# First norm of a two-block forward pass: the shift enters as one-row products ahead of the transposes, and start-up transfers are asked for in another order

## The reference, cut to what matters

```python
mod = jax.nn.silu(c) @ w_ada[l] + b_ada[l]
shift1, scale1, gate1, shift2, scale2, gate2 = jnp.split(mod, N_MOD, axis=-1)
h = modulate(rms_norm(x, norm1_g[l]), shift1, scale1)     # h * (1 + scale1) + shift1
proj = h @ w_in[l]
```

## Time and profile before

| | us |
|---|---|
| three runs, median | 1350.91 |
| lowest and highest | 1350.15 and 1354.35 |
| the profiled execution | 1351.17 |
| its span from first to last instruction | 1349.4 |
| PE busy | 1214.6 (90%) |
| DVE busy | 554.2 (41%) |
| ACT busy | 452.0 (33%) |

### The profile page before, as it was taken

One profiled execution on the slowest core, in us unless ns is written; L12 is line 12 of the kernel. 1 busy time (PEld: TensorE's weight loads), 2 busy tenths in 40 slices (PEclk: granted clock), 3 DMA queues, 4 the chain that ended last, 5 costly groups with the idle time before them and its releaser, 6 DMA issues.

```text
span 1349.4 us, 16311 instructions
## 1 busy us (share of the span) xinstructions
PE 1214.6 (90%) x6501; PEld 841.4 (62%) x6504; DVE 554.2 (41%) x805; ACT 452.0 (33%) x657; POOL 45.6 (3%) x66
## 2 busy tenths in 40 slices
PE   3799999879799789969999869999989988899998
PEld 0677677765344335424554328888879866688886
DVE  0545545674111112211121146464456654544444
ACT  1345445242111112201222134444445544444443
POOL 1000000000000000000000020020010001000000
PEclk9799999979899889979999979999999978899999
DMA  9986565548999999999999996555525106355540
GB/s 345 374 292 241 217 222 185 209 165 331 376 422 420 393 422 421 421 387 422 421 421 421 417 331 196 187 187 187 198 100 187 63 1 210 122 199 189 187 152 32
DMA packets 115087, 360.03 MB, mean 267 GB/s; under 512 B 14995, under 2 KB 62404, under 8 KB 83980
## 3 DMA queue, kind: packets, MB, share of 16 engines
q1 hardware_dynamic: 113360, 352.71, 69.1%
q10 hardware_dynamic: 1340, 2.94, 0.6%
q0 software_dynamic: 320, 3.46, 0.6%
HBM read 355.89 MB, written 4.50 MB: 267 GB/s over the span
## 4 chain that ended last, share of the span: by engine, by line
PE 80%; DMA 9%; DVE 5%; ACT 3%; issue 1%; POOL 1%; SPq 1%; ACTq 0%; DVEq 0%; POOLq 0%
PE bank L1943 30%; PE bank L2120 16%; PE bank L2047 9%; DMA ring<-in_w_up_e 6%; PE bank L2145 5%; PE bank L1994 5%; PE bank L2097 3%; PE bank L2157 3%; DMA att<-in_buckets 1%; PE bank L2212 1%; DMA raw_g<-in_w_in 1%; PE bank L1959 1%; PE bank L2234 1%; DVE g_lo L1243 1%; PE bank L2036 1%
## 5 line engine op out<-in xcount | busy, mean ns | idle before, releaser
L1243 DVE TENSOR_TENSOR g_lo<-raw_g,g_hi 128x2048 fp32r<-128x2048 f32 (+2 forms) x88 | 201.8, 2295 | 119.1 <-ACT g_hi L798 62.4
L2120 PE MATMUL bank<-ring,xg 128*64 128x512 f32 (+1 forms) x1152 | 211.9, 636 | 41.6 <-DMA ring<-in_w_up_e 41.6
L1943 PE MATMUL bank<-g_hi,xt_hi 128*128 128x512 f32 (+1 forms) x592 | 240.1, 406 | 5.8 <-DVE xt_lo L1859 2.2
L1943 PE MATMUL bank<-g_hi,xt_lo 128*128 128x512 f32 (+1 forms) x592 | 232.7, 393 | 0.0
L1943 PE MATMUL bank<-g_lo,xt_hi 128*128 128x512 f32 (+1 forms) x592 | 232.4, 392 | 0.0
L2120 PEld LDWEIGHTS bank<-ring,xg 128*64 128x64 f32 (+1 forms) x1152 | 65.6, 133 | 184.5 <-issue 184.5
L1943 PEld LDWEIGHTS bank<-g_hi,xt_hi 128*128 128x128 f32 x592 | 113.0, 191 | 35.7 <-issue 10.2
L1943 PEld LDWEIGHTS bank<-g_hi,xt_lo 128*128 128x128 f32 x592 | 112.6, 190 | 24.1
L1943 PEld LDWEIGHTS bank<-g_lo,xt_hi 128*128 128x128 f32 x592 | 112.9, 191 | 21.2
L2145 PE MATMUL bank<-ring,a_t 128*64 128x512 f32 (+1 forms) x576 | 102.2, 597 | 1.4 <-DVE pickT L1346 0.9
L1388 DVE SCALAR_TENSOR_TENSOR arena<-arena,w_row_of,bank 128x256 f32<-128x256 f32 x28 | 13.5, 481 | 218.4 <-ACT arena L918 214.3
(11 more groups left out here) (347 smaller groups left out, 1579.9 us busy)
## 6 DMA issues: line engine op xcount, KB each, us to landing
ring<-in_w_gate_e SPq DMA_DIRECT2D x64, 1024.0 KB, 12.5
ring<-in_w_up_e SPq DMA_DIRECT2D x64, 1024.0 KB, 16.5
ring<-in_w_down_e SPq DMA_DIRECT2D x64, 1024.0 KB, 15.5
raw_g<-in_ffn_w_gu SPq DMA_DIRECT2D x44, 1024.0 KB, 8.5
raw_g<-in_w_in SPq DMA_DIRECT2D x26, 1024.0 KB, 7.0
raw_d<-in_ffn_w_down SPq DMA_DIRECT2D x22, 1024.0 KB, 4.9
ada_d<-in_w_ada SPq DMA_DIRECT2D x16, 1024.0 KB, 5.0
raw_g<-in_w_out SPq DMA_DIRECT2D x8, 1024.0 KB, 5.1
```

The source lines that it names most:

```text
L1243: dve.tensor_tensor(lo, raw, hi.bitcast(F32), ALU.subtract).then_inc(S.lo_g, 1)
L1943: last = pe.matmul(out_, src[s][:, c, b * P:(b + 1) * P], w((g_hi, g_lo)[m], i), start=start and i == 0 and k == 0, stop=stop and i == len ...
L2120: last = pe.matmul(bank(4)[r, :].rearrange("p (g n) -> p g n", g=2), xg[:, s // 2 % 2, c, at_:at_ + r.stop - r.start], gate_up_raw(pair, j ...
```

## The change

The shift is no longer spread and added by DVE. `ada_spread` spreads scale1 alone, into banks 6 and 7. A new `first_transposes` first puts the shift into banks 0 to 3, already transposed: for each of 16 blocks of 128 x 128, two products of one row of `mod_rows` (64 columns of the stationary side) with a row of ones. Then it adds h to them by 16 plain products with the identity, where the old code used transposes. DVE only scales.

The transfers: on ACT's queue `con`, the gain and `g2_rows` are asked for after the third piece of `w_ada` has landed and ahead of the squares of x; the two small tables and `b_ada` come ahead of x. On POOL's queue `t_scratch` waits until group 0 of `w_in` has been split and `n_scratch` until the last group has.

```diff
             pool.wait_ge(tb_sb, 1)
             pool.dma_start(t_one, t_bias).then_inc(in_["t1"], 16)
-            pool.wait_ge(in_["t1"], 16)
-            pool.dma_start(t_dram, t_one.unsqueeze(0).to_broadcast([P, NH, BX])).then_inc(in_["tw"], 16)
-
             link(pool.memset(rpb_pad, 0.0))
...
             pool.dma_start(n_one, rpb_pad).then_inc(in_["n1"], 16)
+            pool.wait_ge(in_["t1"], 16)
+            pool.wait_ge(M.lo_g, 2 * G_WIN + 2)
+            pool.dma_start(t_dram, t_one.unsqueeze(0).to_broadcast([P, NH, BX])).then_inc(in_["tw"], 16)
             pool.wait_ge(in_["n1"], 16)
+            pool.wait_ge(M.lo_g, 2 * (G_WIN + N_WIN - 1) + 2)
             pool.dma_start(n_dram, n_one.unsqueeze(0).to_broadcast([64, NH, NR])).then_inc(in_["nw"], 16)
...
             act.dma_start(c_col, a["c"].rearrange("o (p c) -> p (o c)", c=DC)).then_inc(in_["c"], 16)
-            act.dma_start(con[:, :], a["con"]).then_inc(in_["con"], 16)
-            act.dma_start(x[:, :, :], a["x"].rearrange("o (b p) n -> p (o b) n", p=P)).then_inc(in_["x"], 16)
             act.dma_start(relb_in[0:32, :], a["rel_bias_t"]).then_inc(in_["relb"], 16)
...
-            act.dma_start(gain1, a["norm1_g"].to_broadcast([P, D])).then_inc(in_["g1"], 16)
-            for j in range(2):
-                act.dma_start(g2_rows[32 * j:32 * j + 32, :], a["norm2_g"][:, j * 512:(j + 1) * 512].to_broadcast([32, 512]))\
-                    .then_inc(in_["g2r"], 16)
+            act.dma_start(x[:, :, :], a["x"].rearrange("o (b p) n -> p (o b) n", p=P)).then_inc(in_["x"], 16)
+
+            def late_loads():
+
+                act.wait_ge(landed_ada[2], 16)
+                act.dma_start(gain1, a["norm1_g"].to_broadcast([P, D])).then_inc(in_["g1"], 16)
+                act.dma_start(con[:, :], a["con"]).then_inc(in_["con"], 16)
+                for j in range(2):
...
             act.activation(c_sil, c_col, ACT.Silu).then_inc(c_silu, 1)
+            late_loads()
             squares(0, [x[:, b, :] for b in range(TB)], in_["x"], 16, lambda i: h[:, i, :])
 
-            act.wait_ge(ada_bc, 4)
-            act.activation(shift1, ps[0][:, :, :].rearrange("p a n -> p (a n)"), ACT.Copy).then_inc(ada_ev, 1)
...
-                dve.wait_ge(ada_bc, 4)
-                src = ps[1][:, :, :].rearrange("p a n -> p (a n)")
+                dve.wait_ge(ada_bc, 2)
+                src = ps[3][:, :, :].rearrange("p a n -> p (a n)")
...
             for b in range(TB):
-                link(scaled(h[:, b, :], x[:, b, :], b, gain1))
-                dve.wait_ge(ada_ev, 1)
-                dve.tensor_tensor(h[:, b, :], h[:, b, :], shift1, ALU.add).then_inc(h_ready, 1)
+                scaled(h[:, b, :], x[:, b, :], b, gain1).then_inc(h_ready, 1)
...
+            def first_transposes():
+
+                def block(q, i):
+                    return bank(q)[:, i * P:(i + 1) * P]
+
+                for q in range(4):
+                    for i in range(4):
+                        for j in range(2):
+                            row = mod_rows[32 * j:32 * j + 1, 4 * (q % 2) + i:512:DC]
+                            pe.matmul(block(q, i)[64 * j:64 * j + 64, :], row, ones[32 * j:32 * j + 1, :],
+                                      start=i == 0, stop=False, skip_group_check=True)
+                pe.wait_ge(in_["con"], 16)
+                for q in range(4):
+                    pe.wait_ge(h_ready, q // 2 + 1)
+                    for i in range(4):
+                        ins = pe.matmul(block(q, i), h[:, q // 2, 4 * (q % 2) + i:D:DC], ident,
+                                        start=False, stop=True, skip_group_check=True)
+                    ins.then_inc(M.xt_ps, 1)
```

More of the change, by code:

```diff
@@ L352, in build @@
         landed_ada_d = [sem("landed_ada_d0"), sem("landed_ada_d1")]
-        ada_used, ada_rows, ada_bc, ada_ev = sem("ada_used"), sem("ada_rows"), sem("ada_bc"), sem("ada_ev")
+        ada_used, ada_rows, ada_bc = sem("ada_used"), sem("ada_rows"), sem("ada_bc")
         tb_ps, tb_sb = sem("tb_ps"), sem("tb_sb")
@@ L783, in _ @@
                     .then_inc(in_["bada"], 16)
-            act.dma_start(gain1, a["norm1_g"].to_broadcast([P, D])).then_inc(in_["g1"], 16)
-            for j in range(2):
-                act.dma_start(g2_rows[32 * j:32 * j + 32, :], a["norm2_g"][:, j * 512:(j + 1) * 512].to_broadcast([32, 512]))\
-                    .then_inc(in_["g2r"], 16)
+            act.dma_start(x[:, :, :], a["x"].rearrange("o (b p) n -> p (o b) n", p=P)).then_inc(in_["x"], 16)
[4 more added lines that the diff above has]
+                for j in range(2):
+                    act.dma_start(g2_rows[32 * j:32 * j + 32, :], a["norm2_g"][:, j * 512:(j + 1) * 512].to_broadcast([32, 512]))\
+                        .then_inc(in_["g2r"], 16)
             def split_hi(g, u, gated_tile=False, it=None, cols=UNIT, S=M, by=2):
@@ L1961, in ada_chunks, with ada_spread @@
                                   skip_group_check=True).then_inc(ada_used, 1)
-            def ada_spread(r):
-                pe.wait_ge(ada_rows, r + 1)
-                for j in range(4):
-                    pe.matmul(bank(j), ones[32 * j:32 * j + 1, :], mod_rows[32 * j:32 * j + 1, :], start=True, stop=True)\
-                        .then_inc(ada_bc, 1)
+            def ada_spread():
+                pe.wait_ge(ada_rows, 1)
+                for j in range(2):
+                    rows_ = slice(32 * (2 + j), 32 * (2 + j) + 1)
+                    pe.matmul(bank(6 + j), ones[rows_, :], mod_rows[rows_, :], start=True, stop=True).then_inc(ada_bc, 1)
+            def first_transposes():
[3 more added lines that the diff above has]
+                    for i in range(4):
+                        for j in range(2):
+                            row = mod_rows[32 * j:32 * j + 1, 4 * (q % 2) + i:512:DC]
[8 more added lines that the diff above has]
+                    ins.then_inc(M.xt_ps, 1)
             def ada_at(j, u):
@@ L2342, in _ @@
             pe.wait_ge(tb_sb, 1)
-            ada_spread(0)
-            pe.wait_ge(in_["con"], 16)
-            transposes(0)
+            ada_spread()
+            first_transposes()
             pe.wait_ge(M.xt_lo, 4)
```

## The result

The changed kernel takes 1356.88 us (median of 20 runs, 1352.19 to 1365.78), the kernel before 1350.78 in 20 runs beside it: a ratio of 1.0038, 95% interval 1.0023 to 1.0054, which is 5.1 us longer (3.1 to 7.3); the two medians differ by 6.1. The forecast was 1346.6 with a range up to 1351.5, and it was wrong in its sign. The profiled run took 1355.2, its span is 1353.2 (before: 1349.4).

A forecast was written before the change was run, and what follows sets the result against it. It took PE, busy 90% of the span, as the bound, so only its idle or low-clock stretches could pay. Dense 1.1 us earlier plus 3.0 from the clock gave 4.1, put at 4.3: 1346.6 us, range 1343.5 to 1351.5.

The forecast's parts named there:

- 16 x 0.22 = 3.5 us at the full clock: PE, first norm: 16 plain products replacing the transposes take 3.5 us, priced at 0.22 us each.
- forecast gain of 4.3: Whole kernel: 4.1 us from the opening and clock, put at 4.3 for a one-third chance of 6.3.
- the rest warm: PE after 3.0 us of cold one-row products: the clock is full, so they end at 42.4 and transposes take 3.5.
- Rival 5: First norm on PE: a plain product costs four transposes, not two, 6.4 us instead of 3.5; 1349.5 us, chance 0.03.
- 5.0 in the sum: PE after the spread: one-row products run from 37.4 to 42.4, the first 3.0 us cold, the rest warm.
- rival 4: One-row products on PE: pairs don't overlap or weight loads wait, 13.6 us; slower at 1355.5 us, chance 0.06.
- From the spread on it has no gap: PE from spread through transposes runs without pause, so the clock rises some 5 us into that run.
- Rival 3: One-row products don't lift PE's clock: they take 7.0 us, plain ones start cold (5.5); gain 0, 1350.9 us, chance 0.16.
- 3.0 us that a warm start was to give: Start of dense work: PE arriving at the full clock saves 3.0 us in the first 6 us.
- The last piece at 30.9: Opening transfers: the last 2 MB piece of w_ada lands at 30.9 instead of 32.4, a gain of 1.5 us.
- rival 2: Opening transfers: w_ada pieces land no earlier, 32.4 as before; gain 2.8 us, 1348.1 us, chance 0.18.
- The last products cold (3.4): PE on the last piece of w_ada: its products run at the low clock and take 3.4 us, to 34.3.

The follow-up runs named there:

- loads_only: The kernel before with only the new order of transfers on ACT's and POOL's queues, old arithmetic kept; 1350.65 us, ratio 0.9992.
- after_warm: The changed kernel with zero products added on PE, 8 ahead of the last two chunks of w_ada and 3 ahead of the spread; 1352.47 us, ratio 1.0012.
- shift_only: The changed kernel's new arithmetic with the old order of all transfers; 1356.79 us, ratio 1.0039 to the kernel before.
- rows_32: The changed kernel with each one-row product replaced by one of 32 equal rows against a tile of 1/32; 1356.96 us, ratio 1.0044.
- contiguous_after: The changed kernel with h written by DVE in chunk order, so plain products load contiguous weights; 1357.75 us, ratio 1.0063.
- contiguous_before: The kernel before with h of the first norm written in chunk order, transposes unchanged; 1357.32 us, ratio 1.0049.
- warm: The kernel before with the two DRAM tables asked for late and zero products keeping PE running through the opening; 1347.95 us, ratio 0.9976.
- best: The kernel before with zero products, x scaled early, scale and shift read from PSUM, small tables ahead of x, con late; 1348.44 us, ratio 0.9975.
- contiguous_tables_fillers: The kernel before with h in chunk order, the two DRAM tables asked for late and zero products on PE; 1351.94 us, ratio 1.0014.

## Why the prediction was wrong, point by point

**The plain products: the term that failed.** The sum took "16 x 0.22 = 3.5 us at the full clock", from the earlier trace rows. They took 7.92 (7.89, 7.90, 7.88 in three other kernels). The factor of two records to one was right; the price of a record was read from products whose weights lie side by side (load of 192 ns, records 0.11 us apart), and here they lie 8 elements apart (336 ns) and the records start 0.24 us apart. That is 4.4 us on the path and by itself turns the forecast gain of 4.3 into nothing. Nor could "the rest warm" help: the pace of these products is the same at both levels. The layout isn't the only reason that 3.5 us were out of reach: with contiguous weights in the same place, mostly cold, they took 6.14, so the low clock alone would have cost 2.6 of the 4.4.

**Rival 5.** The rival of a plain product at four transposes put it at 0.40. The runs show that the rule of the Trainium skill ("TensorE: Matmul & The Clock Gate", section Terms: transpose mode is four times faster for FP32) depends on the layout: at the full clock a strided plain product takes two records of 0.24 and a strided transpose one of 0.12, a factor of four; contiguous it is two of 0.11 to one of 0.11, a factor of two; and strided and cold two of 0.24 to one of 0.21, little over two. The prediction set the rule aside by a row with another layout. Its rival gave 1349.5 with 0.40 us a product, and the true price was higher still, 0.48. In its comparison it also read the 1.59 us of eight transposes as cold; part of them lies in 44 to 45, where the earlier trace rows has 0.92, and eight wholly cold ones took 1.94 and 1.97 in `loads_only`.

**The one-row products.** 5.91 us against 5.0 in the sum (37.4 to 42.4, 3.0 of it cold), 5.25 in `after_warm`, 7.10 and 7.11 wholly cold in `shift_only` and `rows_32`. The price was right (a record every 0.11 us cold and 0.06 warm, two side by side), and pairs do overlap: rival 4's mechanism, records one after another for 13.6 us, is false, and that its time of 1355.5 is the nearest to the result is luck. What failed here is the clock.

**The clock.** "From the spread on it has no gap", so the clock was to rise in some 5 us. It fell instead, at full load. Rival 3 had this, and had its consequence wrong: the cold clock costs the plain products nothing, since they don't get faster when warm. In the changed kernel the clock does arrive full at 50 to 52, and PE then waits 1.41 us for the last split. It is back at 0.50 soon after; `after_warm` and `contiguous_after` have the same wait and stay at 1.00, so what decides it isn't shown. The first whole microsecond of dense work, beside the 0.50 of 48 to 54 in the earlier trace rows:

```profile
53.00:54.00 1.00, 1.00 (x5) 0.54 0.02 8
```

The prediction also read from 44 to 45 of the earlier trace rows that transposes lift the clock, against the Trainium skill ("TensorE: Matmul & The Clock Gate", the part on PE-mode transpose). `loads_only` has the same 16 transposes in the same rhythm, and its clock after them is

```profile
44.00:45.00 1.00, 0.58 (x4) 0.50 0.98 410
45.00:46.00 1.00, 1.00 (x5) 0.50 0.98 410
```

and `contiguous_before` stays at 0.50 as well. One execution speaks for the rise, two for the skill's rule: the reading stood on too little, and the runs don't settle it.

Of the 3.0 us that a warm start was to give, about 1.3 came: the records of dense work are 0.21 apart until 56.4, 3.5 us, instead of 6.

**The transfers.** The last piece at 30.9 was wrong: 32.27, 31.7 to 32.2 in the other kernels with the new order. That is rival 2, "pieces no earlier" (32.4). The last products cold (3.4) were right (3.37). g_hi at 37 was right (36.85), the squares at 27 to 29 nearly (29.28), and PE waited for neither con nor the gain. The spread took 1.13 and not 2.0: the clock was full from 36 on, where the sum had it cold.

**The sum with the measured terms.** Last piece 32.3, products 3.4, addition and waits 1.0, spread 1.1: 37.8. One-row products 5.8: 43.6. Plain products 7.9: 51.5. The last xt_hi and xt_lo 1.4: 52.9. Against before, dense counted as if warm: 52.9 + 1.7 - (48.3 + 3.0) = 3.3, and the trace has 3.4 at the first product with `att`. The forecast had 47.2, warm; 54.6 is what the trace has by that reckoning. The 7.4 between are 1.4 of the last piece, 0.8 of one-row products, 4.4 of plain products, 0.1 at the end and 1.7 of clock, less 1.0 in the spread and the addition. Its gain of 4.1 less 7.4 is the loss of 3.3. (The 4.3 that the prediction took as its gain doesn't follow from its own chances: 4.1, with a third of a chance of 6.3, gives 4.8.)

**What was right.** The opening ends with the first dense product, and what is saved or lost there reaches the next stages (3.3 by the sum, 3.4 at 106). A warm start is worth about 3 us: `warm` starts dense 0.5 us later than before and gains 3.2 (1.8 to 4.9), and in its trace 2.1 at 106.

## What to carry to other kernels

Before PE takes over work of another engine, price its records by a row with the same mode and the same layout of the weights: here the same 128 x 128 block cost 0.12 us as a transpose and 0.48 as a plain product at the full clock, and the row of 0.22 was of contiguous weights. A busy PE isn't a warm one: under one-row products on 64 columns of weights the clock fell at full load, and 32 rows didn't raise it, while products of zeros over the whole array, put where PE would stand still, kept it up for most of the opening and won 3 us without touching the arithmetic. Look at what follows a saved stretch: here the chains of DVE and of `w_in` were shortened as planned, and neither was what ended last any more.

## What the runs showed of the hardware that was not expected

- The weight load of a plain fp32 product with elements 8 apart takes 336 ns at both levels of the clock (1.2 and 2.4 GHz), and its records start 0.24 us apart at both; with contiguous weights it is 333 and 192 ns, 0.21 and 0.11 us. In transpose mode at the full clock the strided load takes 193 to 196 ns (`best`, `warm`), the contiguous one 140 (`contiguous_tables_fillers`).
- The granted clock fell from 1.00 to 0.50 while PE was busy with one-row products in three kernels (3.00 of 3.00 us in the changed one), and 7.1 us of them or of 32-row ones didn't raise it.
- Zeros in bf16 over the full array hold the clock: in `best` it is 1.00 from 30.2 past the first dense products. That they raise it isn't shown so plainly. In `best`, 3.64 us of `w_ada` products stand right before them, and in `after_warm` the clock was full at 28.2, before the first zeros at 28.55. In `warm` it rose at 47.7 under zeros that had run since 45.49, behind transposes.
- The clock column shows 1.00 where the trace holds no record of the clock. In the changed kernel the first record is at 29.2 us; in 25 to 28 the column has 1.00 while 16 records took 3.64 us, the pace of the low level. The pace of known records is the safer sign.
- DVE writing 128 x 1024 fp32 elements 128 apart took 1.90 to 2.00 us a pass instead of 1.2 to 1.3 (`contiguous_before`).
- In its order behind the small loads x took 25.0 us to land instead of the 15.4 of the earlier trace rows, and the last piece of `w_ada` was there only 0.15 us earlier (0.15 to 0.75 in all kernels with the new order), over 8 MB.
